# A hybrid encoder block: the first pass's order of keys, banks and outputs, and the opening's conditioning sums taken one column group at a time

## The chip, the cores and the metric

The kernel runs on one core of a Trainium2 chip. The metric is the device time of one execution in microseconds. TensorE (PE) does the matrix products, VectorE (DVE), ScalarE (ACT) and GpSimd (POOL) the elementwise work, and SyncE (SP) issues the transfers. Each engine takes its instructions in order and waits on semaphores that the others raise. A PSUM bank holds 128x512 float32; there are eight of them, numbered 0 to 7.

## What is computed

One encoder block on x (512 tokens, 1024 features), with a conditioning vector c of 1024 values:

```python
mod = c_act @ w_ada[l] + b_ada[l]
sh1, sc1, g1, sh2, sc2, g2 = [t[:, None, :] for t in jnp.split(mod, 6, axis=-1)]
h = rms_norm(x, norm1_gain[l]) * (1.0 + sc1) + sh1
x = x + g1 * token_mixer(h, w_in[l], conv_w[l], q_gain[l], k_gain[l], sink[l], w_o[l])
h = rms_norm(x, norm2_gain[l]) * (1.0 + sc2) + sh2
x = x + g2 * conv_ffn(h, w_up[l], ffn_conv_w[l], ffn_conv_b[l], w_down[l])
```

The token mixer projects h to B, C, u (a gated convolution of width 3), q, k, v (16 query and 4 key heads of 64 features; a token attends to others within 128, with a distance bias and a sink logit per head) and two gates. The two branches are gated, added and projected once more. The second half is a gated convolution FFN of inner width 2816.

## The kernel before

Every float32 product is made of three float32r products: a matrix is split into a high part (ACT rounds it) and a low part (POOL or DVE subtracts), and PE adds high*high, high*low and low*high in one bank. A 128-row block of features is a "tile"; a "pair" is two tiles (256 columns) of a weight matrix.

**The opening** (to some 57 us). x arrives and is transposed by PE (L845) into xT; ACT copies the banks out (L571). The tokens' 1/rms is spread over a bank by a product with ones (L850), and ACT copies it to SBUF (L609, `r_copy`). POOL multiplies each tile of xT by it (L486) and makes the low parts of that row's key/value weights (L476, `kv_l`) and query weights (L478, `q0_l`). The scale and shift of a tile come from c_act and w_ada. `gemv0(i, ks)` adds, on DVE (L1195), c_act[k]*w_ada[k] for the two tiles 2i and 2i+1, shift and scale at once (512 columns), over k = 0 to 7; ACT does the product for k = 0 (`first_product`, L596) but for i = 0. `mod_turn(i)` on PE (L861) transposes the 512 sums, `mods(i)` on DVE (L1203 to L1210) reduces them to the columns mod and amp, and then ACT writes h_hi of a tile and a float copy (L584, L588), and DVE subtracts for h_lo (L1216). PE takes row t of the queries' first pair and of all keys and values as tile t of h comes: 4 query products (L872, L873), 8 key/value products (L880, L881), 2 query products with h_lo (L884), 4 key/value products with h_lo (L888). `mod_turn(1)`, `(2)`, `(3)` stand inside rows t = 1, 3 and 5. DVE's order in the opening is thus: sums, mods, h_lo, sums, h_lo, sums, once per two tiles. The small parameters (b_ada, gains, convolution weights) are 10 transfers into `par_rows` (`par_in`) and one for the sinks, issued by SP between the first and second of its key/value loads; PE transposes them (L854), ACT copies them to `par` (L613, `par_c`).

**The four passes** (57 to some 390 us), g = 0 to 3. In each, six pairs (five in the last) go in the order C U B A Q G. A pair's first tile is computed in bank 0 and its second in bank 1. One half of a tile's products (12 products) is a slot: slots 0 to 3 are C, 4 to 7 U, and so on. Hand-written tables (SCORE, TURN, K_TURN, Q0_TURN) say before which slot PE does the attention's steps, and ACT and DVE go through the same slots:

- `query(0, u)` (ACT, L636 and L639) and `query_low` (DVE, L1245) take the first queries out of banks 0 and 1 behind the opening. PE's C of pass 0 waits for them.
- The keys are normalised by DVE (L1297) into `k_n`, in the buffer prob, then turned by PE (`key_turn`, L917) and split by ACT (L657) and DVE (`key_low`, L1311). prob is also what the scores are written to.
- `scores(b, ...)` (PE, L964) for block b of queries, taken by DVE (`take`, L1326); two banks, so that heads 2 and 3 wait until heads 0 and 1 are taken. Then `shift`, exp on ACT, `row_factors`, normalisation on ACT, transposes on PE (`turn`, L975), split (`pt_hi` on ACT, `pt_lo` on DVE, L1347), the product with v (`values`, L992, bank 6), and `heads_low` (ACT, L693) and `heads_out` (DVE, L1356), which empty bank 6 one slot after `pv_slot(g, b)`, the slot of b's last product.
- `gemv(g, k)` (DVE, L1277 and L1283) adds the conditioning sums of the later stages, one k behind each of the even slots 4 to 18. Their input `ada` is loaded by SP between the loads of the weight pairs. SP loads pair n only when POOL has finished the low part of pair n-2.

**The rest** (w_o, the second norm, the FFN) is not touched.

## Time and profile before

| | us |
|---|---|
| median of 3 runs | 806.92 (805.38 to 809.6) |
| the profiled execution | 808.3 |
| its span, first to last instruction | 806.2 |
| PE busy in it | 774.8 |
| DVE, ACT, POOL busy in it | 515.6, 374.2, 374.2 |

The profile's page gives shares of the whole. What counts here are the first 150 us, so the timeline of each engine there, the list of waits and tables by stretches of time are read. In a timeline row, several instructions of one kind are one row with their count; the brackets at the end tell how long the engine had been idle and what ended that. Matmul durations in it overlap: a row of four products may last longer than the distance to the next.

### The profile page before, as it was taken

How to read it: one execution, taken by the hardware profiler on the slowest of the kernel's cores; microseconds unless marked ns; L12 is line 12 of the kernel's file. 1: busy time of each engine (PE TensorE's matmuls, PEld its weight loads, DVE VectorE, ACT ScalarE, POOL GpSimd, SP SyncE). 2: the span in 40 equal slices, each digit the busy share in tenths (PEclk: the TensorE clock that was granted, in tenths of full speed). 3: DMA queues.
4: the chain of work that ended last, by engine and by line, in shares of the span. 5: the costliest groups of instructions: out<-in, count | busy, mean ns of one | idle time of the engine just before them, and what ended most of it. 6: DMA issues, size and time to landing. Idle time of an engine off the chain costs nothing.

```text
span 806.2 us, 10380 instructions
## 1 busy us (share of the span) xinstructions
PE 774.8 (96%) x3709; PEld 644.4 (80%) x3709; DVE 515.6 (64%) x722; ACT 374.2 (46%) x664; POOL 374.2 (46%) x223
## 2 busy tenths in 40 slices
PE   3889999999999999999999999999999999999997
PEld 3677787788888888878889988888888888888886
DVE  5847876658765976686638799888888988000000
ACT  7665467455654575556524454434443343112220
POOL 2774423343453345244863255554444555444340
PEclk9999999999999999999999999999999999999999
DMA  8943342243414341533143042223333322323311
GB/s 301 381 146 116 134 155 78 72 164 131 158 54 181 131 157 52 184 130 108 57 150 105 4 154 85 75 100 104 104 104 104 98 75 76 104 92 118 131 52 40
DMA packets 83279, 96.03 MB, mean 119 GB/s; under 512 B 2674, under 2 KB 77610, under 8 KB 83242
## 3 DMA queue, kind: packets, MB, share of 16 engines
q1 hardware_dynamic: 79018, 93.44, 34.0%
q10 hardware_dynamic: 4224, 2.10, 0.8%
q8 instruction: 23, 0.38, 0.2%
q14 instruction: 14, 0.11, 0.0%
HBM read 93.43 MB, written 2.10 MB: 118 GB/s over the span
## 4 chain that ended last, share of the span: by engine, by line
PE 85%; DVE 9%; ACT 3%; issue 2%; DMA 1%; SPq 0%; DVEq 0%
PE bank L832 25%; PE bank L833 25%; PE bank L834 25%; PE bank L964 2%; PE bank L992 2%; PE bank L975 2%; DVE acc L1283 1%; DVE bank L1195 1%; DVE pt_lo L1347 1%; DMA ada<-in_w_ada_dram 1%; DVE a_buf L1371 1%; DVE sm L1333 1%; DVE prob L1326 1%; PE bank L881 1%; PE bank L880 1%
## 5 line engine op out<-in xcount | busy, mean ns | idle before, releaser
L832 PE MATMUL bank<-h_hi,w_hi 128*128 128x512 f32 (+1 forms) x760 | 294.8, 388 | 2.3 <-DVE q_st L1245 2.3
L833 PE MATMUL bank<-h_lo,w_hi 128*128 128x512 f32 (+1 forms) x760 | 292.4, 385 | 0.0
L834 PE MATMUL bank<-h_hi,w_lo 128*128 128x512 f32 (+1 forms) x760 | 292.2, 384 | 0.0
L450 POOL TENSOR_TENSOR w_lo<-w_raw,w_hi 128x1024 fp32r<-128x1024 f32 x76 | 194.8, 2585 | 195.4 <-ACT w_hi L546 188.1
L457 POOL TENSOR_TENSOR w_lo<-w_raw,w_hi 128x512 fp32r<-128x512 f32 x88 | 123.8, 1428 | 181.1 <-ACT w_hi L546 181.1
L546 ACT ACTIVATE w_hi<-w_raw 128x1024 fp32r<-128x1024 f32 x120 | 122.5, 1052 | 100.4 <-PE bank L834 100.4
L832 PEld LDWEIGHTS bank<-h_hi,w_hi 128*128 128x128 f32 x760 | 143.4, 189 | 30.0 <-issue 2.7
L834 PEld LDWEIGHTS bank<-h_hi,w_lo 128*128 128x128 f32 x760 | 143.6, 189 | 28.7
L833 PEld LDWEIGHTS bank<-h_lo,w_hi 128*128 128x128 f32 x760 | 143.7, 189 | 26.5
L832 PE MATMUL bank<-g_hi,w_hi 128*128 128x512 f32 x176 | 69.2, 393 | 0.0
L834 PE MATMUL bank<-g_hi,w_lo 128*128 128x512 f32 x176 | 68.6, 390 | 0.0
L833 PE MATMUL bank<-g_lo,w_hi 128*128 128x512 f32 x176 | 68.5, 389 | 0.0
L685 ACT ACTIVATE pt_hi<-bank 128x512 fp32r<-128x512 f32 x40 | 22.1, 593 | 59.4 <-PE bank L975 59.3
L1283 DVE SCALAR_TENSOR_TENSOR acc<-ada,c_act,acc 128x1024 f32<-128x1024 f32 x28 | 44.1, 1576 | 0.4
L787 ACT ACTIVATE pad_f<-bank 128x512 f32<-128x512 f32 x22 | 13.1, 599 | 66.1 <-PE bank L834 66.1
L1326 DVE SCALAR_TENSOR_TENSOR prob<-bank,sm,bias 128x256 f32<-128x256 f32 (+1 forms) x64 | 32.1, 542 | 17.5 <-PE bank L964 17.5
L671 ACT ACTIVATE prob<-prob,sm 128x256 f32<-128x256 f32 (+1 forms) x64 | 35.2, 555 | 14.1 <-DVE sm L1336 14.1
L1557 DVE TENSOR_TENSOR g_lo<-y_buf,g_hi 128x512 f32 x22 | 37.9, 1720 | 4.3 <-DVE g_hi L1556 3.0
L1565 DVE SCALAR_TENSOR_TENSOR y_buf<-bank,mod,xT 128x512 f32<-128x512 f32 x4 | 3.0, 751 | 58.7 <-PE bank L834 58.7
L834 PEld LDWEIGHTS bank<-g_hi,w_lo 128*128 128x128 f32 x176 | 33.0, 188 | 7.0
L1347 DVE TENSOR_TENSOR pt_lo<-bank,pt_hi 128x512 fp32r<-128x512 f32 x40 | 26.1, 685 | 19.5 <-ACT pt_hi L685 19.5
L832 PEld LDWEIGHTS bank<-g_hi,w_hi 128*128 128x128 f32 x176 | 33.1, 188 | 6.7
(186 smaller groups left out, 1056.9 us busy)
## 6 DMA issues: line engine op xcount, KB each, us to landing
w_raw<-in_w_in_dram SPq DMA_DIRECT2D x23, 1024.0 KB, 5.1
w_raw<-in_w_up_dram SPq DMA_DIRECT2D x21, 1024.0 KB, 4.9
ada<-in_w_ada_dram SPq DMA_DIRECT2D x32, 512.0 KB, 6.0
ada<-in_w_ada_dram SPq DMA_DIRECT2D x32, 256.0 KB, 6.3
w_raw<-in_w_down_dram SPq DMA_DIRECT2D x8, 1024.0 KB, 4.7
...
```

The costliest lines, as they stand in the source:

```text
L450: pool.tensor_tensor(lo_of(n, u), raw(n)[:, :, u * P:(u + 1) * P], hi_of(n, u), SUB).then_inc(lo_ready, 1)
L457: ins = pool.tensor_tensor(lo_of(n, u)[:, k, :], raw(n)[:, k, u * P:(u + 1) * P], hi_of(n, u)[:, k, :], SUB)
L546: act.activation(hi_of(n, u), raw(n)[:, :, u * P:(u + 1) * P], ACT.Copy).then_inc(hi_ready, 1)
L671: act.activation(prob[:, b % 2, h, 0:w], prob[:, b % 2, h, 0:w], ACT.Exp, bias=sm[:, 1, b, h:h + 1], accum_out=sm[:, 3, b, h:h + 1]).then_ ...
L685: act.activation(pt_hi[:, t % 2, :], bank[TB[t % 2]][:, :], ACT.Copy).then_inc(pt_h, 1)
L832: pe.matmul(dst, w_h, rhs_hi, start=first, stop=False)
L833: pe.matmul(dst, w_h, rhs_lo, start=False, stop=False)
L834: return pe.matmul(dst, w_l, rhs_hi, start=False, stop=last)
L1283: dve.scalar_tensor_tensor(acc[:, :], ada[:, k % 2, :], c_act[:, 0, k:k + 1], acc[:, :], MUL, ADD).then_inc(ada_done, 1)
L1326: dve.scalar_tensor_tensor(prob[:, b % 2, h, 0:w], bank[SC[h % 2]][:, 0:w], sm[:, 6, b, h:h + 1], bias[:, h, c0:c0 + w], MUL, ADD).then_in ...
L1347: dve.tensor_tensor(pt_lo[:, t % 2, :], bank[TB[t % 2]][:, :], pt_hi[:, t % 2, :], SUB).then_inc(t_free, 1)
L1557: dve.tensor_tensor(lo, y_buf[:, u, :], hi, SUB).then_inc(ffn_tiles, 1)
```

## The change

1. **Opening, sums by column group.** The sums of tiles 0 and 1 are no longer made together. `gemv_tile(u, ks)` makes those of tile u: 8 instructions of 2x128 columns each, all on DVE; `mod_turn_tile(u)` makes two transposes, `mods_tile(u)` reduces them. Tile 0's scale is raised on its own semaphore. Groups 1 to 3 stay as they were.
2. **Opening, orders.** The 11 small transfers are issued by POOL instead of SP. PE turns them before it turns x's tiles 4 to 7, and ACT copies them there; ACT makes the first row's key/value and query weights (`start_high(0)`) behind the copies of xT instead of ahead of them. POOL's first three scaled tiles go to a buffer of their own, `n_first`, so that they needn't wait until x is fully transposed. In the last row PE does the two query products with h_lo ahead of the keys' blocks 2 and 3.
3. **Unit bank.** The first tile of pass 0's C goes to bank 6 (`unit_bank`); the wait for the queries of banks 0 and 1 moves to C's second tile and to U's first. ACT takes C's first tile out before the v copies.
4. **Keys.** `k_n` lies in the buffer merged. K_TURN is {4: (0,), 6: (1,), 7: (2,), 8: (3,)} instead of {3: (0,), 4: (1, 2), 5: (3,)}. The second half of the first queries' norm sums, their root and their norm go to slots 4 and 5. POOL's low part of the third pair starts one half of a key block earlier, and in four pieces instead of two.
5. **Sums of pass 0.** The gemv steps k = 1 to 7 stand two even slots later (slots 10 to 22).
6. **Outputs' bank.** heads_low and heads_out stand at `pv_slot(g, b)`, not one slot behind, in all four passes.

```diff
-        K_TURN = {3: (0,), 4: (1, 2), 5: (3,)}
+        K_TURN = {4: (0,), 6: (1,), 7: (2,), 8: (3,)}
+        Q0_NORM = 5
-        GEMV_AT = {n + 1: n for n in range(KT)}
+        GEMV_AT = [{n + 1 + (2 if n else 0): n for n in range(KT)}] + [{n + 1: n for n in range(KT)}] * (KV - 1)
...
+        def unit_bank(n, u):
+            return bank[OB if (n, u) == (P_MIX + 1, 0) else u][:, :]
...
+            parameters()
             pool.wait_ge(r_copy, 1)
-            pool.wait_ge(xt_done, KT)
             for t in range(KT):
+                if t == 3:
+                    pool.wait_ge(xt_done, KT)
                 pool.wait_ge(xt_out, t + 1)
-                pool.tensor_tensor(hT[:, t, :], xT[:, t, :], a_buf[:, 0, :], MUL).then_inc(xr_pool, 1)
+                pool.tensor_tensor(hT[t], xT[:, t, :], a_buf[:, 0, :], MUL).then_inc(xr_pool, 1)
                 start_low(t)
...
-            pool.wait_ge(kn_ready, 1)
-            low(None, 0, P_MIX + 2)
+            pool.wait_ge(kn_half, 1)
+            for u in range(2):
+                low_by_halves(P_MIX + 2, u)
...
                 pe.wait_ge(kv_l, t + 1)
                 for b in range(NB):
+                    if b == 1 and t == 0:
+                        pe.wait_ge(h_ready, 1)
+                        mod_turn_tile(1)
...
+                    if b == 2 and last:
+                        query_low_row()
...
-                    if kind == "C" and not g or kind == "G" and g < KV - 1:
+                    if not g and (kind, u) in (("C", 1), ("U", 0)) or kind == "G" and g < KV - 1:
...
+            def gemv_tile(u, ks):
+                def by_tile(v):
+                    return v.rearrange("p (s n) -> p s n", s=2)[:, :, u * P:(u + 1) * P]
+                for k in ks:
+                    dve.wait_ge(ada0_in[k // 2], 32)
+                    src = ada0[:, k // 2, k % 2, :, u * P:(u + 1) * P]
...
+                    dve.scalar_tensor_tensor(by_tile(bank[MB][:, :] if k < KT - 1 else acc0[:, :]), src,
+                                             c_act[:, 0, k:k + 1], by_tile(bank[MB][:, :]), MUL, ADD).then_inc(gemv_done, 1)
...
+                if t == 0:
+                    gemv_tile(1, range(2))
+                    mods_tile(0)
+                    gemv_tile(1, range(2, 5))
+                    h_low(0)
+                    gemv_tile(1, range(5, KT))
+                    gemv0(1, range(1, 3))
+                    mods_tile(1)
+                    gemv0(1, range(3, 5))
...
-                        if slot == pv_slot(g, b) + 1:
+                        if slot == pv_slot(g, b):
                             heads_out(b)
```

DVE in the opening, from the sums of the first group to the first row of the second, before. st is the tokens' variance; L1203 to L1210 are `mods`.

```order
L1195 SCALAR_TENSOR_TENSOR acc<-ada,c_act,bank 128x512
L1225 SCALAR_TENSOR_TENSOR amp<-par 128x8
L1203 TENSOR_REDUCE bank<-bank 128x4
L1207 TENSOR_TENSOR mod<-bank,par 128x2x2
L1210 SCALAR_TENSOR_TENSOR amp<-bank,par,amp 128x1 x2
L1195 SCALAR_TENSOR_TENSOR bank<-ada,c_act,bank 128x512 x2
L1216 TENSOR_TENSOR h_lo<-bank,h_hi 128x512
L1195 SCALAR_TENSOR_TENSOR bank<-ada,c_act,bank 128x512 x2
L1216 TENSOR_TENSOR h_lo<-bank,h_hi 128x512
```

The same stretch of DVE after (L1242 and L1232 are the sums of one tile, L1220 those of a group, L1250 to L1254 `mods_tile`).

```order
L1284 SCALAR_TENSOR_TENSOR amp<-par 128x8
L1232 TENSOR_SCALAR bank<-ada,c_act 128x2x128
L1242 SCALAR_TENSOR_TENSOR bank<-ada,c_act,bank 128x2x128
L1250 TENSOR_REDUCE bank<-bank 128x2
L1253 TENSOR_TENSOR mod<-bank,par 128x2
L1254 SCALAR_TENSOR_TENSOR amp<-bank,par,amp 128x1
L1242 SCALAR_TENSOR_TENSOR bank<-ada,c_act,bank 128x2x128 x3
L1275 TENSOR_TENSOR h_lo<-bank,h_hi 128x512
L1242 SCALAR_TENSOR_TENSOR bank<-ada,c_act,bank 128x2x128 x2
L1242 SCALAR_TENSOR_TENSOR acc<-ada,c_act,bank 128x2x128
L1220 SCALAR_TENSOR_TENSOR bank<-ada,c_act,bank 128x512 x2
L1250 TENSOR_REDUCE bank<-bank 128x2
```

Eight instructions of tile 1 now stand between the scale of tile 0 and the sums of group 1, and the second `mods_tile` stands behind two sums of group 1.

DVE behind the opening, from the keys' values to the first scores, before (L1297 makes k_n, L1252 the query sums, L1303 the low part of v, L1311 `key_low`, L1277 the first gemv step, L1326 `take`; L1164 to L1167 are a norm).

```order
L1297 TENSOR_TENSOR prob<-bank,st 128x4x64 x8
L1252 TENSOR_REDUCE st<-bank 128x4x2
L1159 TENSOR_SCALAR st<-st 128x16
L1303 TENSOR_TENSOR v_st<-bank,v_st 128x4x64 x4
L1164 RECIPROCAL st<-st 128x16
L1165 SCALAR_TENSOR_TENSOR st<-st 128x16
L1166 TENSOR_TENSOR st<-st 128x16
L1167 SCALAR_TENSOR_TENSOR sm<-st 128x16
L1311 SCALAR_TENSOR_TENSOR k_st<-bank,c_act,k_st 128x512 x3
L1277 TENSOR_SCALAR acc<-ada,c_act 128x1024
L1311 SCALAR_TENSOR_TENSOR k_st<-bank,c_act,k_st 128x512
L1326 SCALAR_TENSOR_TENSOR prob<-bank,sm,bias 128x256 x4
```

The same place after.

```order
L1365 TENSOR_TENSOR merged<-bank,st 128x4x64 x8
L1370 TENSOR_TENSOR v_st<-bank,v_st 128x4x64 x4
L1377 SCALAR_TENSOR_TENSOR k_st<-bank,c_act,k_st 128x512
L1320 TENSOR_REDUCE st<-bank 128x4x2
L1188 TENSOR_SCALAR st<-st 128x16
L1345 TENSOR_SCALAR acc<-ada,c_act 128x1024
L1193 RECIPROCAL st<-st 128x16
L1194 SCALAR_TENSOR_TENSOR st<-st 128x16
L1195 TENSOR_TENSOR st<-st 128x16
L1196 SCALAR_TENSOR_TENSOR sm<-st 128x16
L1392 SCALAR_TENSOR_TENSOR prob<-bank,sm,bias 128x256 x2
L1377 SCALAR_TENSOR_TENSOR k_st<-bank,c_act,k_st 128x512
```

The queries' norm has moved from before the keys to behind the first gemv step, and three of the four key steps stand among or behind the first scores.

## Rows read from the trace of the kernel before

**Rows 1.** The page: the span.

```profile
span 806.2 us, 10380 instructions
```

**Rows 2.** PE's waits: line and releaser, total us, times, longest.

```profile
PE bank L872 <- ACT h_hi L584: 2.8, 1, 2.8
PE bank L992 <- DVE y_buf L1356: 2.7, 2, 1.7
PE bank L832 <- DVE q_st L1245: 2.3, 1, 2.3
...
PE bank L964 <- DVE prob L1326: 2.0, 1, 2.0
...
PE bank L917 <- DVE k_st L1311: 1.4, 1, 1.4
```

**Rows 3.** By stretches: length, busy PE, PEld, DVE, ACT, POOL, granted clock, DMA.

```profile
60.00:65.00 5.00, 5.00 (x17) 4.00 (x18) 2.84 (x5) 3.41 (x9) 0.05 (x1) 0.66 0.25 86
...
97.30:103.00 5.70, 5.70 (x20) 4.51 (x21) 5.31 (x9) 0.00 (x0) 2.93 (x3) 0.70 0.71 254
```

**Rows 4.** PE's timeline: start, us, line, idle time before it.

```profile
22.22 0.47 PE L872 MATMUL bank<-h_hi,w_hi 128*128 128x512 f32 x1 [2.79 <-ACT h_hi L584]
...
28.19 0.63 PE L861 MATMUL bank<-ident,acc 128*128 128x128 f32 x4 [0.27 <-DVE acc L1195]
...
37.31 0.63 PE L861 MATMUL bank<-ident,acc 128*128 128x128 f32 x4 [0.28 <-DVE acc L1195]
...
56.61 1.07 PE L888 MATMUL bank<-kv_hi,h_lo 128*128 128x512 f32 x4
```

**Rows 5.** DVE's timeline in the opening.

```profile
13.66 4.20 DVE L1195 SCALAR_TENSOR_TENSOR bank<-ada,c_act,bank 128x512 f32<-128x512 f32 x5
17.97 0.75 DVE L1195 SCALAR_TENSOR_TENSOR acc<-ada,c_act,bank 128x512 f32<-128x512 f32 x1
18.74 0.83 DVE L1225 SCALAR_TENSOR_TENSOR amp<-par 128x8 f32<-128x8 f32 x1
...
27.30 0.75 DVE L1195 SCALAR_TENSOR_TENSOR acc<-ada,c_act,bank 128x512 f32<-128x512 f32 x1
```

**Rows 6.** DVE's groups by shape: count, total us, mean ns.

```profile
L1326 DVE SCALAR_TENSOR_TENSOR prob<-bank,sm,bias 128x256 f32<-128x256 f32 x32 | 13.9, 476 | 3.8 <-PE bank L964 3.8
...
L1203 DVE TENSOR_REDUCE bank<-bank 128x4 f32<-128x512 f32 x4 | 2.8, 699 | 2.5 <-PE bank L861 2.4
...
L1479 DVE TENSOR_REDUCE st<-bank 128x2 f32<-128x256 f32 x2 | 0.8, 424 | 0.5 <-PE bank L1067 0.5
```

**Rows 7.** ACT's timeline in the opening.

```profile
18.59 2.08 ACT L571 ACTIVATE xT<-bank 128x512 f32<-128x512 f32 x4
```

**Rows 8.** POOL's timeline in the opening.

```profile
3.82 0.51 POOL L471 TENSOR_SCALAR_AFFINE_SELECT ndist<-ndist 128x384 f32<-128x384 f32 x1
18.27 1.28 POOL L486 TENSOR_TENSOR x_nat<-xT,a_buf 128x512 f32<-128x512 f32 x1 [13.95 <-PE bank L845]
19.51 1.26 POOL L476 TENSOR_TENSOR kv_lo<-b_buf,kv_hi 128x512 fp32r<-128x512 f32 x1
20.74 0.72 POOL L478 TENSOR_TENSOR w_lo<-w_raw,w_hi 128x256 fp32r<-128x256 f32 x1
```

**Rows 9.** SP's last small transfer, and its transfers' KB and median us to landing.

```profile
13.81 0.35 SPq L363 DMA_DIRECT2D sink_b<-in_sink_dram  x1
...
sink_b<-in_sink_dram SPq DMA_DIRECT2D x1, 8.0 KB, 4.2
```

**Rows 10.** Behind the opening: POOL, SP and DVE, then DVE again (timelines).

```profile
67.42 4.75 POOL L450 TENSOR_TENSOR w_lo<-w_raw,w_hi 128x1024 fp32r<-128x1024 f32 x2 [7.37 <-DVE prob L1297]
...
72.60 1.05 SPq L411 DMA_DIRECT2D ada<-in_w_ada_dram  x2
...
78.36 0.75 DVE L1277 TENSOR_SCALAR acc<-ada,c_act 128x1024 f32<-128x1024 f32 x1
...
94.20 2.42 DVE L1283 SCALAR_TENSOR_TENSOR acc<-ada,c_act,acc 128x1024 f32<-128x1024 f32 x1
```

More of the change, by code:

```diff
@@ L116, in encoder_block @@
         kv_lo = sb("kv_lo", [P, KT, 2 * PC], f32r, into=start)
+        n_first = sb("n_first", [P, 3, S], into=start)
         start.close()
@@ L708, in _ @@
                             key_high(j)
+                    if g == 0 and slot == Q0_NORM:
+                        root(None, 0, 2, NB * HG, 1, 2)
                     for b in range(NB):
@@ L881, in _ @@
                     pe.matmul(kv_bank(b), h_hi[:, t, tokens], kv_lo[:, t, :], start=False, stop=False)
[L882 to L886 removed]
+                if not last:
+                    query_low_row()
                 for b in range(NB):
```

139 lines of the change are left out of this document (83 added, 56 removed).

## The prediction, made before the changed kernel was run

> **What bounds the kernel now.** The span is 806.2 us in a profiled execution of 808.3, so 2.1 us lie around it [rows 1]; PE is busy for 774.8 of it. So only two things can be won: time in which PE stands still, and time in which it runs at the lower clock. The list of PE's waits comes first. Four of its entries lie where the change works: 2.8 us before the first product of the opening, 2.3 us behind the opening, where C of pass 0 waits until the first queries are out of banks 0 and 1, 1.4 us for a key step, 2.0 us for the first take of block 1, and 2.7 us in two waits for bank 6 (1.7 and 1.0) [rows 2]. The table by stretches adds what a wait can bring with it: of 60.00 to 65.00 the granted clock is 0.66, of 97.30 to 103.00 it is 0.70 [rows 3]. Between 2.4 GHz and 1.2 GHz (a clock of 0.5) that is 0.34 x 5.00 = 1.7 us and 0.30 x 5.70 = 1.7 us lost. Both stretches follow the waits of 2.3 and 2.0 us; none of the waits of 1.7 us and less is followed by one.
>
> The opening is read engine by engine. PE begins at 22.22 and ends its last row at 56.61 + 0.9, call it E = 57.5 [rows 4]. Between, it waits 0.27 and 0.28 us, both for DVE's acc: the sums of groups 1 and 2 are ready at 28.05 [rows 5] and just before 37.31, one group every 37.31 - 28.19 = 9.12 us. PE and DVE are thus nearly equal there, DVE a little the slower. A delay in DVE's sums is a delay of E, and nothing behind it gives it back.
>
> **The opening's sums: a loss.** A sum of 512 columns follows the last every (17.97 - 13.66) / 5 = 0.86 us and lasts 0.75 [rows 5], so 0.11 lies between two of them. The same operation from PSUM on 256 columns lasts 0.476 [rows 6]; with the 0.11 a sum of one tile takes 0.585. Half the columns take two thirds of the time, since a fixed part stays.
> Tile 0: eight of these end at some 16.9 (start as before with the transfer; three ahead of the variance, five behind), 1.9 us earlier than acc before. That is not worth it, because the next on DVE is amp (L1225), which needs the parameters and was 0.83 us long for 8 columns: it ended at 19.57, when POOL's multiplication (18.27 + 1.28 = 19.55) did [rows 5, 8]. POOL now begins that multiplication when the 1/rms is copied, at about 17.3, and amp ends with it at 18.6, 1.0 us earlier.
> From there to the sums of group 1, before 28.05 - 19.57 = 8.5 us, DVE has more to do: 8 x 0.585 = 4.7 us for tile 1, and a second mods: two reductions of 0.42 for one of 0.70 [rows 6] and a further pair of small operations of some 0.3, so 0.4. ACT's first product of group 1 can no longer be done in advance, as bank 7 holds tile 1's sums until then; DVE stands for 0.8. The small waits for PE's transposes about balance. Sum: 18.6 + 8.5 + 4.7 + 0.4 + 0.8 = 33.0, against 28.05: **5.0 us later**. If a tile's sum took only half of 0.86, 0.43, it would be 1.2 less; if 0.7, 0.9 more. Both ends are for the range.
> Does PE begin earlier? Its first product needs h_hi and the low query weights of row 0. On ACT the four copies of xT (2.08 us [rows 7]) now stand ahead of start_high(0): they run from 17.5 to 19.6, the weights are rounded by 20.4, h_hi by 21.5. POOL's two low parts follow the rounding and take 1.26 and 0.72 [rows 8]: 20.2 to 22.2. PE begins at 22.2, as before. n_first thus frees POOL for work that isn't there yet. And PE's early products don't count: it waits within row 0 for tile 1's sums, before row 1 for h_hi, and within row 1 some 2.7 us (from 30.4 to 33.1) for group 1.
> That last wait is longer than the 2.3 and 2.0 us behind which the clock fell. PE's products behind it decide the rest of the opening with DVE's, so a stretch at 1.2 GHz costs up to the 1.7 us of [rows 3], less the 0.28 of slack [rows 4]; it can also lie partly in the wait itself. I take **1.2**, the range is 0 to 1.7.
>
> **The parameters on POOL: a small loss.** Ten transfers must have landed when PE reaches their transposes at about 16.4, now ahead of x's tiles 4 to 7. POOL is free for them at 3.82 + 0.51 = 4.3 [rows 8]. No row shows POOL issuing a transfer. The nearest from below is SP's 0.35 each, from above an operation of POOL of 1.28 [rows 8, 9]; landing takes 4.2 [rows 9]. Ends: 4.3 + 3.5 + 4.2 = 12.0, in time, and 4.3 + 12.8 + 4.2 = 21.3, 4.9 late. I take 0.9 each, as POOL's own rows are the nearer kin: 17.5, 1.1 late. Up to 0.6 is hidden by POOL's multiplication, so **0.5**; at the late end all but 0.6 goes into the chain. SP saves 11 x 0.35 = 3.9 us of issues, which brings nothing: DVE has no wait for a transfer behind the first.
> The Trainium skill, DMA: Bandwidth & Descriptors, in the section on latency and other measured facts, gives some 0.6 us to the first byte for a transfer from SP or ACT and some 1 us for one from GpSimd, whose own cores write the descriptors; with 1.0 us for each issue the parameters would be 2.1 us late and the loss 1.5 instead of 0.5. No row of this trace shows it.
>
> **Behind the opening: the gain.** With C's first tile in bank 6, PE goes on at E. The two query products ahead of four others put the queries' end 0.9 us earlier; by the pace of before their low parts are ready at E + 3.1, and C's second tile starts at E + 5.9. So the wait of 2.3 and its slow clock of 1.7 are gone, and no other wait is near: POOL's low weights of pair 1 are ready before E, as before. The key step at slot 4 finds k_n done at E + 9.1 (the wait of DVE for the query sums falls away), and the second and third have two and three slots; the 1.4 is gone. The 2.0 before slot 10 came from DVE, which had two gemv steps between the first and second block's takes, the last of 2.42 us [rows 10]. Both are moved behind slot 10; three key steps come in, each about as long as the 0.75 of [rows 10]. DVE is then, by my count, some 0.7 us ahead of PE there, so the 2.0 and the 1.7 of clock go too. Together 2.3 + 1.7 + 1.4 + 2.0 + 1.7 = **9.1**.
> What is late next: gemv step 0 now stands ahead of the queries' norm. Its data come behind pair 4, which SP loads only when POOL has finished pair 2. Before, POOL began that at 67.42 and was done at 72.17, SP went on at 72.60, and DVE took the step at 78.36 [rows 10], so up to 6.2 us from POOL's end. POOL now begins at E + 6.5, ends at E + 11.5; the data are there at E + 17.4 or so. DVE would be ready at E + 14.5, and waits; with the step (0.75) and the norm (four small dependent operations, an estimate of 0.9) take(0) begins at E + 19.0, its first head is out at E + 19.5, and PE wants the bank at E + 18.8. That is a **new wait of 0.7** (0 to 1.8).
> Later gemv steps delay their loads and SP's queue behind them; pair 8's load goes from slot 17 to 18, its rounding is at slot 22. The last step ends some 2 us ahead of PE's turn of the sums in pass 1. Nothing.
>
> **The outputs' bank.** In pass 0 heads_low(1) comes out at slot 17, where ACT is idle, 5 us earlier: the wait of 1.7 goes. The wait of 1.0 at block 3 stays: there ACT has the second queries and a table load ahead, and what PE then waits for is pt_lo behind the moved gemv step. **1.7**, between 0.7 and 2.7. Passes 1 to 3 have hardly a wait for this bank, and I take 0.
>
> **Sum.** 9.1 - 0.7 + 1.7 = 10.1 won, 5.0 + 1.2 + 0.5 = 6.7 lost: **3.4 us less**. The profiled execution would be 808.3 - 3.4 = 804.9, and the median, 1.4 below it before, 806.9 - 3.4 = **803.5**.
>
> **Rivals.**
> (a) The opening's loss is only the sums' 5.0: parameters in time, the lower clock inside the wait. For: the first 2.8 us wait at 22.22 was followed by full clock. Against: both waits of 2.0 and more in dense work were not. 803.5 - 1.7 = 801.8. Chance 0.30.
> (b) DVE's chain isn't what decides the opening: a tile's sum takes well under 0.5 us and PE begins near 20. For: acc of tile 0 is ready 1.9 us earlier. Against: the 0.28 waits for acc and the row of 0.476. Loss 2 instead of 6.7: 798.8. Chance 0.12.
> (c) Slower: POOL's issues. PE's transposes of x's tiles 4 to 7 stand behind the parameters now, so all of h waits for them. At 1.28 us each the loss is 4.3 instead of 0.5, and the time 807.3; from there on it is slower than before, and at 2 us each (28.5 us for the last to land, 12 late, a loss of 11.5) 814.5. Beyond 1.6 us each it is slower by over 0.5%. For: no row shows POOL issuing any. Against: ten small transfers, and POOL has nothing else from 4.3 to 17. Chance 0.13.
>
> **How the numbers follow.** The forecast has 0.45, (a) 0.30, (b) 0.12, (c) 0.13. What a measurement of this kernel can tell from no change is about 0.5%, 4.0 us, so faster begins below 802.9: that is (a) and (b) and, less what of (a) lies above, together 0.42. Slower, above 810.9, is half of (c) and a little for the unseen, 0.08. The rest is 0.50. The range takes in (a), most of (b) and (c) to 808.5; it begins at 798.5. The likeliest case's own range, by its terms' ends, is 801 to 806.5.
>
> **What the profile after would show.** PE's first product at 22 +- 1; its wait for acc at 33 (28.19 before) of over 2 us, the last row's end at 63 to 65; a granted clock below 1 between 30 and 40. No wait of PE between the last row and slot 6, and there one of under 2 us for take(0), with DVE waiting for the ada transfer. No clock loss behind it. If PE's last row ends before 60, or POOL's issues end after 17, the sum is wrong in that term.

## The result, and the profile after

The changed kernel takes 816.03 us (median of 4 runs, 812.84 to 817.96) against 807.33 us for the kernel before (4 runs, 805.38 to 809.6): a ratio of 1.0103, interval 1.0067 to 1.0139. It is slower by 1.0%; forecast were 3.4 us less. The profiled execution took 817.96 us, and its page answers [rows 1] thus (busy us, share of the span, instructions):

```profile
span 815.8 us, 10398 instructions
...
PE 782.3 (96%) x3709; PEld 648.8 (80%) x3709; DVE 519.5 (64%) x732; ACT 375.3 (46%) x664; POOL 385.6 (47%) x236
```

PE is busy 7.5 us longer with the same number of instructions, since it runs at the lower clock more often: its trace has six slow stretches where before has two, the end of the kernel left aside. POOL is busy 11.4 us longer (385.6 against 374.2), though its arithmetic is the same: its 11 transfers are 5.8 of it. The other 5.6 are operations that took longer. DVE has 3.9 more, with ten more instructions. The list of PE's waits answers [rows 2]: us in total, times, the longest.

```profile
PE bank L993 <- DVE prob L1392: 6.0, 4, 3.3
PE bank L1021 <- DVE pt_lo L1413: 4.2, 4, 2.8
PE bank L890 <- POOL w_lo L468: 3.0, 1, 3.0
...
PE bank L872 <- DVE acc L1220: 2.1, 1, 2.1
```

The 2.3 for the queries, the 1.4 for a key step, the 2.0 for the first take of block 1 and the 1.7 for bank 6 are gone, as forecast; the 1.0 at block 3 is 0.84 for pt_lo, as forecast too. New are 3.3 and 1.73 for the scores' banks (L993) and, in pass 3, 2.8 for pt_lo (L1021), where before waits 1.62 in the same place. The table by stretches answers [rows 3] (length, PE busy and its instructions, granted clock, share of the DMA engines, GB/s). Of each stretch the last column but two is the granted clock: a part of it ran at 1.2 GHz, the rest at 2.4.

```profile
32.00:38.00 6.00, 4.77 (x16) 0.72 1.10 386
85.00:90.00 5.00, 5.00 (x19) 0.66 0.40 136
155.00:165.00 10.00, 6.65 (x25) 0.83 0.46 159
360.00:370.00 10.00, 7.20 (x27) 0.83 0.63 210
```

Each of them follows one of the long waits of PE, and each of the last three costs (1 - 0.66) x 5.00 = 0.17 x 10.00 = 1.7 us.

To see where the time went, the same product of PE, counted along PE's instructions, was sought in both traces. It starts later (+) or earlier (-) than in the trace of before by so many us. The columns are places, by the time of before: the last product of the opening, the values of block 2 of pass 0, just behind the second scores of pass 1 (the boundary of passes 0 and 1), the scores of block 0 in pass 2 and in pass 3, behind pass 3, the end. The experiments follow in the same table. Each row is one execution, so a slow stretch more or less moves it by 1.7 us; what an edit is worth is told by the ratios below.

| kernel | 57.3 | 134.9 | 160.9 | 239.7 | 321.1 | 395.9 | 802.4 |
|---|---|---|---|---|---|---|---|
| after | +6.2 | -1.5 | +4.4 | +5.2 | +6.0 | +9.6 | +9.7 |
| e1 | +5.9 | +0.1 | +0.2 | +0.2 | +0.3 | +0.3 | +0.3 |
| e2 | +5.5 | -3.9 | +0.6 | +0.7 | +0.7 | +0.7 | +0.7 |
| e3 | +5.4 | -3.1 | -1.7 | -0.9 | -0.1 | +3.5 | +3.5 |
| e4 | +4.2 | -5.2 | +2.0 | +2.7 | +3.4 | +5.5 | +5.5 |
| e5 | +5.5 | -4.0 | +0.2 | +0.3 | +0.3 | +0.3 | +0.3 |
| e6 | +4.3 | -5.3 | -4.6 | -4.5 | -4.5 | +0.2 | +0.2 |
| e7 | +3.4 | -6.0 | -1.5 | -1.5 | -1.6 | -1.5 | -1.5 |
| e8 | +2.9 | -6.3 | -6.1 | -6.1 | -6.1 | -6.0 | -6.0 |
| e9 | +4.2 | -1.1 | -1.1 | -1.1 | -1.0 | -1.0 | -1.0 |
| e10 | +3.1 | -6.3 | -5.6 | -5.5 | -5.5 | -5.5 | -5.5 |
| e11 | 0.0 | -7.5 | -7.3 | -7.3 | -7.3 | -7.3 | -7.3 |
| e12 | +0.4 | -8.9 | -8.7 | -8.7 | -8.7 | -8.7 | -8.7 |
| e13 | +1.8 | -9.0 | -8.8 | -8.8 | -8.8 | -8.8 | -8.8 |
| e14 | +6.5 | -1.6 | +4.2 | +5.1 | +5.8 | +9.5 | +9.5 |
| e15 | +1.9 | -0.8 | -0.8 | -0.9 | -0.7 | -0.7 | -0.7 |
| e16 | +0.6 | -7.6 | -7.8 | -7.7 | -7.6 | -7.6 | -7.6 |
| e17 | +4.5 | -6.3 | -6.1 | -6.0 | -6.0 | -6.0 | -6.0 |
| e18 | +2.6 | -8.2 | -8.1 | -8.0 | -8.0 | -8.0 | -8.0 |

The row of after shows where the time went. The opening loses 6.2 us (6.7 were forecast), and at 134.9 PE is 1.5 us ahead: a gain of 7.6 us behind the opening. That is 2.5 short of the forecast 10.1 (point 3 below). Then 5.8 us go at the boundary of passes 0 and 1, 1.6 up to pass 3, and 3.6 in pass 3, where the sum had 0.

**The boundary.** First DVE in the trace of after (start us, us, engine, line, operation; merge is L1455 and L1456), then POOL, then PE:

```profile
151.89 1.29 DVE L1351 SCALAR_TENSOR_TENSOR acc<-ada,c_act,acc 128x1024 f32<-128x1024 f32 x1
153.09 1.78 DVE L1455 SCALAR_TENSOR_TENSOR b_buf<-b_buf,y_buf 128x512 f32<-128x512 f32 x1
154.90 1.66 DVE L1456 SCALAR_TENSOR_TENSOR merged<-b_buf,a_buf 128x512 f32<-128x512 f32 x1
156.49 1.76 DVE L1455 SCALAR_TENSOR_TENSOR b_buf<-b_buf,y_buf 128x512 f32<-128x512 f32 x1
158.28 1.63 DVE L1456 SCALAR_TENSOR_TENSOR merged<-b_buf,a_buf 128x512 f32<-128x512 f32 x1
159.84 0.86 DVE L1392 SCALAR_TENSOR_TENSOR prob<-bank,sm,bias 128x256 f32<-128x256 f32 x2
```

```profile
152.05 7.31 POOL L447 TENSOR_TENSOR w_lo<-w_raw,w_hi 128x512 fp32r<-128x512 f32 x4 [4.16 <-ACT w_hi L555]
```

```profile
160.46 1.19 PE L993 MATMUL bank<-k_st,q_st 128*128 128x256 f32 x4 [3.35 <-DVE prob L1392]
```

The four merges take 6.8 us while POOL makes four low parts without a pause. Behind them come the takes for which PE waits 3.35 us. In the trace of before the four took 1.35, 0.69, 0.69 and 0.69: POOL's work there came in two pairs with a pause between them, and only the first merge met one (merge is L1389 and L1390 there):

```profile
151.50 1.35 DVE L1389 SCALAR_TENSOR_TENSOR b_buf<-b_buf,y_buf 128x512 f32<-128x512 f32 x1
152.88 0.69 DVE L1390 SCALAR_TENSOR_TENSOR merged<-b_buf,a_buf 128x512 f32<-128x512 f32 x1
```

```profile
149.76 2.53 POOL L457 TENSOR_TENSOR w_lo<-w_raw,w_hi 128x512 fp32r<-128x512 f32 x2 [3.21 <-ACT w_hi L546]
155.80 2.83 POOL L457 TENSOR_TENSOR w_lo<-w_raw,w_hi 128x512 fp32r<-128x512 f32 x2 [3.50 <-ACT w_hi L546]
```

### The profile page after: what moved, and what is told of

Its sections match the earlier page's. It is cut to its first block, busy times and chain, and to the rows that moved or that the text cites. A ratio compares the mean times of both kernels' runs of the same rounds, so it can differ in the third digit from the quotient of the medians.

```text
span 815.8 us, 10398 instructions
## 1 busy us (share of the span) xinstructions
PE 782.3 (96%) x3709; PEld 648.8 (80%) x3709; DVE 519.5 (64%) x732; ACT 375.3 (46%) x664; POOL 385.6 (47%) x236
## 4 chain that ended last, share of the span: by engine, by line
PE 80%; DVE 8%; ACT 4%; issue 3%; POOL 3%; DMA 2%; SPq 0%; DVEq 0%; ACTq 0%; POOLq 0%
PE bank L844 23%; PE bank L845 23%; PE bank L846 23%; PE bank L993 2%; DMA ada<-in_w_ada_dram 2%; PE bank L1021 2%; POOL w_lo L447 1%; PE bank L1004 1%; DVE acc L1351 1%; DVE pt_lo L1413 1%; POOL k_st L522 1%; PE bank L912 1%; PE bank L911 1%; DVE b_buf L1455 1%; DVE prob L1392 1%
## 5 line engine op out<-in xcount | busy, mean ns | idle before, releaser
L440 POOL TENSOR_TENSOR w_lo<-w_raw,w_hi 128x1024 fp32r<-128x1024 f32 x74 | 191.7, 2610 | 185.4 <-ACT w_hi L555 185.4
L447 POOL TENSOR_TENSOR w_lo<-w_raw,w_hi 128x512 fp32r<-128x512 f32 x92 | 132.3, 1461 | 188.9 <-ACT w_hi L555 184.6
L1392 DVE SCALAR_TENSOR_TENSOR prob<-bank,sm,bias 128x256 f32<-128x256 f32 (+1 forms) x64 | 32.1, 543 | 20.1 <-PE bank L993 19.9
L1351 DVE SCALAR_TENSOR_TENSOR acc<-ada,c_act,acc 128x1024 f32<-128x1024 f32 x28 | 40.9, 1459 | 0.5
L1413 DVE TENSOR_TENSOR pt_lo<-bank,pt_hi 128x512 fp32r<-128x512 f32 x40 | 26.1, 684 | 19.7 <-ACT pt_hi L695 19.6
L845 PEld LDWEIGHTS bank<-g_lo,w_hi 128*128 128x128 f32 x176 | 33.1, 188 | 6.7
```

What stands on the lines that cost most here:

```text
L440: pool.tensor_tensor(lo_of(n, u), raw(n)[:, :, u * P:(u + 1) * P], hi_of(n, u), SUB).then_inc(lo_ready, 1)
L447: ins = pool.tensor_tensor(lo_of(n, u)[:, k, :], raw(n)[:, k, u * P:(u + 1) * P], hi_of(n, u)[:, k, :], SUB)
L845: pe.matmul(dst, w_h, rhs_lo, start=False, stop=False)
L1351: dve.scalar_tensor_tensor(acc[:, :], ada[:, k % 2, :], c_act[:, 0, k:k + 1], acc[:, :], MUL, ADD).then_inc(ada_done, 1)
L1392: dve.scalar_tensor_tensor(prob[:, b % 2, h, 0:w], bank[SC[h % 2]][:, 0:w], sm[:, 6, b, h:h + 1], bias[:, h, c0:c0 + w], MUL, ADD).then_in ...
L1413: dve.tensor_tensor(pt_lo[:, t % 2, :], bank[TB[t % 2]][:, :], pt_hi[:, t % 2, :], SUB).then_inc(t_free, 1)
```

## The experiments

Each kernel ran beside runs of the kernel before. The edits are against the changed kernel or, where it is said, against the kernel of another experiment. The first four undo one part each.

**e1, part 6 undone.**

```diff
-                        if slot == pv_slot(g, b):
+                        if slot == pv_slot(g, b) + 1:
                             heads_low(b)
...
-                        if slot == pv_slot(g, b):
+                        if slot == pv_slot(g, b) + 1:
                             heads_out(b)
```

> The changed kernel with part 6 undone: heads_low and heads_out again one slot behind pv_slot, in all four passes; all else as changed (816.0 us median, ratio 1.010). Theory A (the order on ACT: at slot 22 of pass 0 heads_low of block 3 stands ahead of the rounding of the next pair, so the low part on POOL and the merges on DVE fall upon one another): the wait of 3.35 us at 160.46 and the slow stretch behind it go, 5.1 us; and if part 6 is also what costs in passes 1 to 3, nearly 5 more. The 1.7 us wait for bank 6 in pass 0 comes back. Together 808 to 812.5 us, ratio 1.001 to 1.006. Theory B (the moved conditioning sums, part 5, do it): the second scores of pass 1 still wait over 3 us, POOL's low parts there still run back to back from 152, and the time is 816 to 818, ratio 1.011 to 1.013. Passes 1 to 3: if part 6 is innocent there, PE still loses some 5 us between 178 us and the end against before.

Measured: ratio 0.9988 (0.9967 to 1.0008), 807.94 us, below even theory A's range. Part 6 costs 1.15%, 9.3 us: more than the whole loss. The 3.35 us wait is gone, the 2.8 for pt_lo is 1.62 as before, and the 1.7 us wait for bank 6 in pass 0 is back. Part 5 was still in, so the moved sums alone don't make the boundary late.

**e2, part 6 in pass 0 alone** (the offset is `(g > 0)` in both lines).

> The changed kernel with part 6 in pass 0 alone; in passes 1 to 3 heads_low and heads_out are again one slot behind pv_slot. If part 6 is what costs 5 us behind 178 us (waits of 2.8, 0.5, 0.5 and 0.3, and a clock of 0.97 between 350 and 400): 811 us, ratio 1.004, with the boundary of passes 0 and 1 as in the changed kernel (wait of 3.35 us). If it is the boundary's late start that runs on: 816, ratio 1.010.

Measured: 1.0022 (1.0001 to 1.0043), less than the 1.004 expected. Passes 1 to 3 now lose nothing (+0.6 and +0.7 in the table), and the boundary, with its wait of 3.35 us, still takes 4.5 us. So part 6 costs in two places: at the boundary and behind it, 0.8% there.

**e3, part 5 undone.**

```diff
-        GEMV_AT = [{n + 1 + (2 if n else 0): n for n in range(KT)}] + [{n + 1: n for n in range(KT)}] * (KV - 1)
+        GEMV_AT = [{n + 1: n for n in range(KT)}] + [{n + 1: n for n in range(KT)}] * (KV - 1)
```

> The changed kernel with part 5 undone: conditioning sums of pass 0 at slots 4 to 18 again. Theory B (gemv(7) at slot 22, 1.29 us ahead of the merges, and gemv(6) ahead of the variance make the boundary late): the 3.35 us wait and its slow clock go (5.1), while the wait of 2.0 before slot 10 and its clock of 1.7 come back, unless key steps now stand elsewhere: 811 to 815, ratio 1.004 to 1.010. Theory A (order of heads_low on ACT): the boundary stays, the 3.7 come on top: 819 to 820, ratio 1.015.

Measured: 1.0057 (1.0034 to 1.0079), within theory B's range. The boundary takes 1.4 us (-3.1 to -1.7) instead of 5.8, and its wait is 1.27 instead of 3.35: step 7 with its 1.29 us is out of the way, and the first merge, which begins 0.17 us ahead of POOL's low parts, takes 0.69. Removing either part 5 or part 6 thus heals most of it, which neither theory A nor B alone says: both only make DVE reach the merges late, and something else makes the merges long.

**e4, the opening of before** (parts 1 and 2 undone; only the order of the last row's query products stays).

> The changed kernel with the opening of before (sums by pairs of tiles, parameters on SP, start_high(0) ahead of the copies, no n_first); only the order of the last row's query products stays changed. If the opening's loss is 6.2 us and is not given back or enlarged behind it: 809.8, ratio 1.0025, and the last row's end at 57.5; the boundary's wait of 3.35 stays, since it belongs to parts 5 and 6. If the boundary's wait comes from where the opening's end lies against the transfers of ada (theory C), it goes too: 804.7, ratio 0.997.

Measured: 1.0041 (1.0024 to 1.0059), 0.6% below the changed kernel. The wait at the boundary is 3.35 us, as expected; theory C falls. The boundary took 7.1 us (-5.2 to +2.0), where after's took 5.8 and e2's 4.5. The wait is the same in all three, and the clock behind it is not (e2, then e4, of 155 to 165; after has 0.83 there, as shown above):

```profile
155.00:165.00 10.00, 6.95 (x34) 1.00 0.59 210
```

```profile
155.00:165.00 10.00, 8.29 (x28) 0.66 0.59 210
```

How far ahead PE is doesn't lengthen the wait: it is 3.35 with PE ahead by 1.5 us (after), 1.6 (e14), 3.9 (e2) and 5.2 (e4).

**e5, part 6 only for blocks 0 to 2 of pass 0** (offset `(g > 0 or b == NB - 1)`).

> The changed kernel, with part 6 kept only for blocks 0 to 2 of pass 0; block 3 of pass 0 and all blocks of passes 1 to 3 one slot later again. With part 6 in all of pass 0 the ratio was 1.0022, PE 3.9 us ahead of before at 134.9 us and 0.4 behind at 157.6. Theory A (block 3's heads_low at slot 22 delays the rounding and with it POOL, so that POOL's low parts fall upon the merges): the gain of 3.9 us stays, ratio 0.997 to 0.998. Theory D (DVE is simply late at the boundary, since PE has got ahead of it; the earlier PE is there, the longer the wait): the wait of 3.35 us shrinks by the 0.8 of heads_low at most, ratio 1.001.

Measured: 1.0010 (0.9988 to 1.0032), the ratio of theory D. The boundary still took 4.2 us (-4.0 to +0.2), 1.7 of them a slow stretch that e2 did not have. The wait is 2.27 instead of 3.35. So the place of block 3's heads is worth 1.1 us of the wait and isn't the whole cause: theory A is refuted as it stands. Theory D's "the earlier PE is there, the longer the wait" doesn't hold either, by e4. POOL's low parts came in two pairs there (148.62 for 2.53 us and 152.08 for 3.16 us), and the merges took 1.41, 0.69, 1.78 and 1.63.

**e6, the changed kernel with POOL held.** POOL's last pair of low parts in passes 0 to 2 is needed by PE only at slot 4 of the next pass:

```diff
                 for i in range(2 * len(kinds(g))):
+                    if g < KV - 1 and i == 2 * len(kinds(g)) - 2:
+                        pool.wait_ge(mix_free, 2 * g + 4)
                     if pair_of(g, i // 2) + 2 <= P_WO:
```

> The changed kernel; in passes 0 to 2 POOL waits with the last pair's low parts until both merges of the pass are done. Needed by PE they are only at slot 4 of the next pass, some 11 us later. If the overlap with POOL is what makes each merge 1.7 us long instead of 0.69 (four of them, 4.0 us), the merges are 0.7 each, the second scores of pass 1 wait under 0.5 instead of 3.35, the slow stretch behind it goes, and the time is 816 less 3.3 less 1.7 = 811, ratio 1.004. If the merges are long for another reason: no change or, by the delay of POOL, 1 us more, ratio 1.010 to 1.012.

Measured: 808.04 us, 1.0010 (0.9982 to 1.0037): 0.9% faster than the changed kernel by one wait of POOL, and 3 us better than expected, as the next two boundaries gain too. DVE and POOL at the boundary (the kernel is two lines longer, so the merge is L1457 and L1458):

```profile
148.04 1.28 DVE L1353 SCALAR_TENSOR_TENSOR acc<-ada,c_act,acc 128x1024 f32<-128x1024 f32 x1
149.24 0.69 DVE L1457 SCALAR_TENSOR_TENSOR b_buf<-b_buf,y_buf 128x512 f32<-128x512 f32 x1
149.96 0.69 DVE L1458 SCALAR_TENSOR_TENSOR merged<-b_buf,a_buf 128x512 f32<-128x512 f32 x1
150.57 0.69 DVE L1457 SCALAR_TENSOR_TENSOR b_buf<-b_buf,y_buf 128x512 f32<-128x512 f32 x1
151.29 0.69 DVE L1458 SCALAR_TENSOR_TENSOR merged<-b_buf,a_buf 128x512 f32<-128x512 f32 x1
151.90 0.87 DVE L1394 SCALAR_TENSOR_TENSOR prob<-bank,sm,bias 128x256 f32<-128x256 f32 x2
```

```profile
152.06 5.02 POOL L447 TENSOR_TENSOR w_lo<-w_raw,w_hi 128x512 fp32r<-128x512 f32 x4 [8.03 <-DVE merged L1458]
```

The order of DVE's instructions is the changed kernel's, to the last one. The four merges take 2.8 us instead of 6.8, and POOL's four low parts 5.02 instead of 7.31. The boundary costs 0.7 us instead of 5.8, and the 1.6 us up to pass 3, which is the same at the next two boundaries, is gone. Each engine stood while the other worked: that is the cause, shown by this edit alone. The takes, whose scores come from PSUM, aren't lengthened: the second pair of e6, at 153.51 beside POOL, took 0.88, and that of after, at 161.26 with POOL idle, 0.91. The Trainium skill, SBUF — State Buffer, section "Who interferes with whom", has the rule: a DVE instruction with two inputs in SBUF contends with a GpSimd instruction that reads SBUF, and such contention is an exclusive lock. The trace agrees, with 1.63 to 1.78 us for 0.69. The prediction had not weighed it.

**e7, blocks 0 to 2 of e5 with the opening of before.**

> The kernel before with parts 3, 4 and 5, the last row's order of query products, and part 6 for blocks 0 to 2 of pass 0 alone: the opening of before. PE was 5.2 us ahead of before at 134.9 us with this opening. By theory A that is kept: 803.5, ratio 0.9935. By theory D the boundary takes back what PE is ahead of DVE there: 807 to 808, ratio 0.998 to 1.000.

Measured: 0.9960 (0.9941 to 0.9979), between the two theories' figures. The boundary took 4.4 us (-6.0 to -1.5), with a wait of 2.26: the same as in e5, though PE is 2.0 us further ahead.

**e8, e7 with POOL held as in e6.**

> The kernel of the run before this one (opening of before, parts 3 to 5, part 6 for blocks 0 to 2 of pass 0) with POOL's last pair of each of the passes 0 to 2 held until the merges are done. If the boundary is bound by merges that POOL lengthens, the ratio is 0.993 whatever block 3 does; if not, as without the wait.

Measured: 801.25 us, 0.9919 (0.9894 to 0.9943). The boundary costs 0.2 us. **e12** is the same kernel again:

> The kernel of e8_best_poolwait once more, on the same chip as the run before this one, in five rounds: 801 us, ratio 0.992 by the theory that PE's gain behind the opening is kept once the merges aren't lengthened. Its last opening product shows again whether the opening of before ends at 57.3 or at 60 to 61.5.

Measured: 802.64 us, 0.9946 (0.9932 to 0.9959), slower than expected, though faster than both kernels again; the intervals of the two overlap.

**e15, the kernel before with POOL held, nothing else.**

> The kernel before with nothing but POOL's wait for the merges in the last pair of passes 0 to 2. Its merges at the boundary of passes 0 and 1 took 1.35, 0.69, 0.69 and 0.69 us and PE waited for nothing there, so holding POOL gains nothing: ratio 0.999 to 1.001. If it is faster by over 0.3%, the lengthened operations cost before too, in a place that the list of waits does not show.

Measured: 0.9992 (0.9966 to 1.0018). The wait is worth nothing in the kernel before, since PE isn't there yet when DVE is. It is worth 0.9%, 7.5 us, in the changed kernel (e6). In e7's it is worth 0.4%, 3.3 us, by e8, and 0.1%, not clear of noise, by e12; the traces of both lose 0.2 us at the boundary where e7's loses 4.4.

**e10, the changed kernel with POOL held, and part 6 undone in pass 3 alone** (offset `(g == KV - 1)`).

> The changed kernel with POOL's wait for the merges (ratio 1.001), and part 6 undone in pass 3 alone. If the 2.8 us wait for pt_lo in pass 3 and the slow clock behind it come from heads_out standing ahead of the takes there, PE keeps the 4.5 us that it is ahead at 320 us: wait 1.6 as before, 4.5 us less, ratio 0.995 to 0.996. If they come from POOL's rounding of another pair falling upon DVE there whatever the heads do: unchanged, 1.001.

Measured: 804.84 us, 0.9972 (0.9955 to 0.9989), 0.4% below e6 and 0.1% above its first case; the 4.7 us of pass 3 (-4.5 to +0.2 in e6) are 0. DVE, POOL and PE in pass 3, of after and then of e10 (again two lines longer: L1439 is the taps' L1437, L1394 the takes' L1392, L1415 pt_lo's L1413):

```profile
355.47 2.45 DVE L1437 SCALAR_TENSOR_TENSOR a_buf<-pad_f,par,a_buf 128x512 f32<-128x512 f32 x2
357.96 2.19 DVE L1351 SCALAR_TENSOR_TENSOR acc<-ada,c_act,acc 128x1024 f32<-128x1024 f32 x1
...
363.50 1.28 DVE L1413 TENSOR_TENSOR pt_lo<-bank,pt_hi 128x512 fp32r<-128x512 f32 x2
```

```profile
355.59 3.47 POOL L447 TENSOR_TENSOR w_lo<-w_raw,w_hi 128x512 fp32r<-128x512 f32 x2 [3.43 <-ACT w_hi L555]
```

```profile
364.24 0.50 PE L1021 MATMUL bank<-pt_hi,v_st 128*128 128x512 f32 x1 [2.80 <-DVE pt_lo L1413]
```

```profile
342.87 1.54 DVE L1439 SCALAR_TENSOR_TENSOR a_buf<-pad_f,par,a_buf 128x512 f32<-128x512 f32 x2
...
345.35 1.86 DVE L1353 SCALAR_TENSOR_TENSOR acc<-ada,c_act,acc 128x1024 f32<-128x1024 f32 x1
...
350.56 1.28 DVE L1415 TENSOR_TENSOR pt_lo<-bank,pt_hi 128x512 fp32r<-128x512 f32 x2
```

```profile
344.83 3.53 POOL L447 TENSOR_TENSOR w_lo<-w_raw,w_hi 128x512 fp32r<-128x512 f32 x2 [4.38 <-ACT w_hi L557]
```

```profile
351.30 0.50 PE L1023 MATMUL bank<-pt_hi,v_st 128*128 128x512 f32 x1 [1.60 <-DVE pt_lo L1415]
```

It is the same cause. In e10 heads_low stands on ACT ahead of the rounding, so POOL starts at 344.83, when the taps (342.87 + 1.54 = 344.41) are over. In after ACT has no heads_low there and rounds 0.8 us sooner, DVE has heads_out ahead of the taps and comes to them later. The taps then meet POOL and take 2.45 instead of 1.54, the sum behind them 2.19 instead of 1.86: 1.24 us together, and PE's wait grows from 1.60 to 2.80, by 1.2. Behind it PE falls to the lower clock, 1.7 us more. (In e4's trace a wait of 2.85 in this place was followed by the full clock.) That the heads' 0.8 us on each engine do this by the collision, and not by themselves, is read from these rows; no run took the collision away in pass 3 alone.

**e9, the opening alone:** the kernel before with parts 1 and 2 and the last row's order.

> The kernel before with parts 1 and 2 alone: the new opening, nothing behind it changed. The prediction priced these at 6.7 us, so 813.6 against 806.9 (ratio 1.008); the trace of the changed kernel had the last row 6.2 us later than the one trace of before. But three traces with the opening of before had the last product at 60.2 to 61.5 (PE ran at the lower clock from about 15 to 29 us in them, and not in the trace of before), and seven with the new opening at 61.6 to 63.5. If before's own trace was an unusually quick opening, the loss is the difference of these means, 2.0 us, ratio 1.0025; if the times of runs are right (4 to 5 us between otherwise equal kernels), ratio 1.005 to 1.006.

Measured: 1.0020 (1.0008 to 1.0032), 1.6 us, near its case of 1.0025. **e17 and e18** differ in the opening alone and ran on one chip; both have parts 3 to 5, POOL's wait, part 6 for blocks 0 to 2 of pass 0 and e13's edit.

> The kernel of e13_gemv0_late_best with the new opening (parts 1 and 2) put back; nothing else differs. Opening alone on the kernel before cost a ratio of 1.002, 1.6 us, where the waits behind it could give some back; here no wait of over 0.7 us is left behind it until 97 us, so the whole price must show. By the 6.7 us of the prediction: 0.9914 + 0.0083, ratio 1.000. By the traces (last product at 57.3 to 61.5 with the old opening, at 60.4 to 63.8 with the new, means 59.2 and 62.5): 3.3 us, ratio 0.995 to 0.996.

> The kernel of e13_gemv0_late_best once more beside the run before this one: 0.991 to 0.993, as the price of the opening is the difference of the two on one chip.

Measured: e17 804.76 us, 0.9974 (0.9958 to 0.9989); e18 800.13 us, 0.9913 (0.9894 to 0.9931). e17 lies between its two cases. The price of the opening is 4.6 us by the medians, 4.9 by the ratios (3 to 7 by their intervals), when nothing behind it can give it back. In the kernel before some is given back. Its wait for the queries is 1.4 us in e9's trace where it was 2.3 in before and in e15, and the clock does not fall behind it; of 60 to 70 (e9, then e15):

```profile
60.00:70.00 10.00, 8.58 (x43) 1.00 0.38 129
```

```profile
60.00:70.00 10.00, 8.09 (x33) 0.83 0.32 106
```

That is 0.9 + 1.7 = 2.6 us of the 4.6, and leaves 2.0, within e9's interval of 0.6 to 2.6.

**e11, e8 with part 2 but without part 1.**

> The fastest so far (ratio 0.992: opening of before, parts 3 to 5, part 6 for blocks 0 to 2 of pass 0, POOL's wait for the merges), and part 2 added: parameters on POOL, transposed ahead of x's tiles 4 to 7, start_high(0) behind the copies of xT, n_first. Part 1 (sums by tile) is left out, so group 0's sums are ready at 18.7 to 19.1 as before. If the orders themselves cost nothing: 0.992, and the parameters' wait before amp (1.36 us in the last trace) goes, up to 1.4 us less, ratio 0.990. If they cost (h_hi and the weights of row 0 come 1.3 us later): 0.994.

Measured: 0.9946 (0.9929 to 0.9963), the same as e12 beside it. Part 2 costs and gains nothing to be seen; what is left of the opening's loss is part 1, the sums by tile, by subtraction, as no run had part 1 alone.

**e13, e8 with conditioning step 0 at slot 8, and e14, the changed kernel with the same edit.**

```diff
-        GEMV_AT = [{n + 1 + (2 if n else 0): n for n in range(KT)}] + [{n + 1: n for n in range(KT)}] * (KV - 1)
+        GEMV_AT = [{n + 3: n for n in range(KT)}] + [{n + 1: n for n in range(KT)}] * (KV - 1)
```

> The kernel of e12_best_again with conditioning step 0 two even slots later too (slot 8 instead of 4), so that DVE no longer waits for its transfer ahead of the first queries' norm. If the wait at slot 6 (1.6 us for prob in that trace) comes from this wait of DVE for ada (3.42 us there): it goes, and with it at times a slow stretch of 1.7 us; 1.6 to 3.3 less, ratio 0.991 to 0.993. If something else is as late (the root on ACT, the norm's four operations): under 0.5 us, ratio 0.994 to 0.995. Steps 1 to 7 and the loads behind them don't move, since the next load waits for step 1.

> The changed kernel with step 0 at slot 8. By the same theory the wait of 1.73 us at 84.31 and the slow stretch behind it go, 3.4 us up to 134.9 us; but with POOL not held the boundary may take what is won there, as it did with the opening. Kept: ratio 1.006; taken back: 1.010.

Measured: e13 799.92 us, 0.9914 (0.9882 to 0.9945); e14 816.73 us, 1.0109 (1.0057 to 1.0160). In e13's trace e12's wait of 1.6 us at slot 6 is gone, so it was step 0; there is a new one of 0.58 at the takes of block 1, ahead of which step 0 now stands. The gain of 1.0 is below what the ratios resolve. In e14 PE won the wait of 1.73 and the slow stretch at slot 6 and lost as much at the takes of block 1, with a wait of 1.71 us and a slow stretch behind it; nothing was left. Taken back, as its second case had it, but earlier than expected, and by a meeting with POOL. Step 0 starts 0.05 us ahead of POOL's low parts in both traces and takes 0.75 us in e13, 1.87 in e14:

```profile
90.37 0.75 DVE L1298 TENSOR_SCALAR acc<-ada,c_act 128x1024 f32<-128x1024 f32 x1
```

```profile
95.08 1.87 DVE L1345 TENSOR_SCALAR acc<-ada,c_act 128x1024 f32<-128x1024 f32 x1
```

**e16, e8 with part 5 undone.**

> The kernel of e12_best_again with part 5 undone (conditioning sums of pass 0 at slots 4 to 18 again). With POOL not held, undoing part 5 gained 3.7 us, since it took gemv(7) out of the way of the merges. If that was all that it gained, and the prediction was right that the sums ahead of block 1's takes cost 2.0 us and a slow stretch of 1.7: slower by 2.0 to 3.7 us than 0.9946, ratio 0.997 to 0.999. If the takes of block 1 are no longer the bound with the keys and banks reordered: 0.994 to 0.995.

Measured: 0.9936 (0.9912 to 0.9959). PE waits 1.12 us for the takes of block 1, with no slow clock behind. Part 5 is worth nothing that can be measured once POOL is held.

## Why the prediction was wrong, step by step

1. **The opening's sums, 5.0: right in the mechanism.** mod_turn(1) was forecast for 33.0 to 33.1 and stands at 33.23, after a wait of 2.15; the slow stretch behind it, for which 1.2 stood in the sum, costs (1 - 0.72) x 6.00 = 1.7; the last row starts at 62.80 (56.61 before), 6.2 us later with that counted:

```profile
23.52 0.58 PE L890 MATMUL bank<-h_hi,w_hi 128*128 128x512 f32 x1 [2.99 <-POOL w_lo L468]
...
33.23 0.63 PE L872 MATMUL bank<-ident,acc 128*128 128x128 f32 x4 [2.15 <-DVE acc L1220]
...
62.80 1.07 PE L916 MATMUL bank<-kv_hi,h_lo 128*128 128x512 f32 x4
```

   Its size against the kernel before is 4.6 to 4.9 us (e17, e18), where 6.7 stood in the sum for the opening as a whole. What was too large is the comparison: the profiled opening of before was a quick one. In nine traces with that opening (before, e4, e7, e8, e12, e13, e15, e16, e18) the last product starts at 57.3 to 61.5, mean 59.3; in ten with the new one at 60.4 to 63.8, mean 62.4. The slow stretch of 32 to 38 is in three of these ten (after, e1, e14).
2. **Parameters on POOL, 0.5: the measured cost is 0.** POOL issued its 11 transfers in 5.8 us, 0.48 to 0.72 each, and was done at 10.44. PE turned the parameters at 16.57 without a wait, and e11 shows no cost. The term took 0.9 each; the 1 us of the page of the Trainium skill named there, DMA: Bandwidth & Descriptors (latency and other measured facts), is for the first byte, and the prediction tried it as the price of an issue in a sentence of its own. Rival (c) fell with it.

```profile
4.63 0.72 POOL L476 DMA_DIRECT2D w_raw<-in_b_ada_dram  x1 [0.31 <-POOL ndist L461]
5.35 1.05 POOL L476 DMA_DIRECT2D w_raw<-in_norm_gain_dram  x2
...
9.87 0.57 POOL L486 DMA_DIRECT2D sink_b<-in_sink_dram  x1
```

3. **The gain behind the opening, 10.1 with bank 6: right in kind.** The waits of 2.3, 1.4, 2.0 and 1.7 and both slow stretches are gone. Up to 134.9 the gain is 7.6. The missing 2.5 are the step "new wait of 0.7": it is 1.73, and the clock falls behind it (0.66 of 85 to 90), which the sum excluded. The clock is this execution's: thirteen traces have a wait of 1.4 to 1.8 at this place, and in ten of them the clock stays up; e2, e5, e6 and e10, whose code up to here is the changed kernel's, gain 9.4 to 9.6.

```profile
82.10 0.75 DVE L1345 TENSOR_SCALAR acc<-ada,c_act 128x1024 f32<-128x1024 f32 x1 [3.55 <-DMA ada<-in_w_ada_dram]
```

```profile
84.31 0.87 PE L993 MATMUL bank<-k_st,q_st 128*128 128x256 f32 x4 [1.73 <-DVE prob L1392]
```

   The data came at 82.1, 18.4 us behind the end of the opening at 63.7, where the sum had 17.4 (its own 11.5 + 6.2 makes 17.7). e13 shows the mechanism. Of the gain, 3.7 were the wait of 2.0 for the take of block 1 with its slow stretch, and most of that was luck of before's trace. The sum of 2.42 us [rows 10] that made it takes 1.28 in e9 and e15, where nothing of this stretch is changed; the wait there is 0.87, at the full clock (e15, whose lines are two later):

```profile
96.13 1.28 DVE L1285 SCALAR_TENSOR_TENSOR acc<-ada,c_act,acc 128x1024 f32<-128x1024 f32 x1
```

4. **"Later gemv steps: Nothing", and "passes 1 to 3: I take 0". These two failed,** and they are the miss: 5.8 us at the boundary, 1.6 behind it, 3.6 in pass 3. Part 6 puts 0.8 us of ACT's and of DVE's work one slot earlier, where they had slack; part 5 puts step 7 (1.29 us) ahead of the merges. Both were priced by their own length alone. What came on top is the neighbour's work: DVE's operations with two SBUF inputs then meet POOL's low parts (e6 by experiment, e10 by its rows). With the meetings at the boundaries taken out by POOL's wait, and those of pass 3 by part 6 undone there, the changed kernel takes 0.9972 (e10), 2.3 us less than before, and its interval of 0.9 to 3.6 us less holds the forecast 3.4. The sign was in the rows of before: a sum of 2.42 us [rows 10], where the same operation takes 1.28 alone, and a merge of 1.35 next to three of 0.69. The first was read as the operation's length (point 3).
5. **"Where a stall goes, what is late next".** Only DVE at slot 6 was asked. The next places where DVE was just in time were the boundaries and pass 3. It isn't PE's lead that made them late (e2, e4, e14: the same 3.35), but the work put ahead of them and its meeting with POOL.
6. **The rivals.** (a) had the opening's 5.0 right (4.6 to 4.9 measured, e17 and e18); (b) and (c) did not happen. The mechanism that made the kernel slower was none of them, and the range ended 7.5 us below the median.

The sum as the traces have it: 6.2 lost in the opening, 7.6 won behind it, 5.8 + 1.6 + 3.6 lost at the boundaries and in pass 3, makes 9.6 of the 9.7 us in the last column; the medians and the ratio say 8.3 to 8.7.

What remains of the change is worth having without its cost. e13's kernel (run again as e18) has the opening of before, parts 3 to 5, step 0 later still, part 6 for three blocks of pass 0, and POOL held at the boundaries: 799.92 and 800.13 us, ratio 0.9914 and 0.9913, faster than both. The largest waits that it still has in the passes (e13):

```profile
PE bank L1013 <- DVE pt_lo L1366: 2.6, 3, 1.6
...
PE bank L985 <- DVE prob L1345: 0.6, 1, 0.6
```

Left open: what parts 3 and 4 are worth each; the two values of e8 and e12, one kernel, stand 0.27% apart, within their intervals.
